# Hybrid attention/MoE layer on one core: the second tile of x is loaded through ScalarE's DMA queue

## What is computed

```python
def rms_norm(x, w):
    y = x * rsqrt(mean(x * x, axis=-1, keepdims=True) + 1e-5)
    return y * w
xn = rms_norm(h, ln1_w)          # h = x, [256, 1024]
proj = xn @ w_in                 # w_in [1024, 8720]
```

## Time and profile before

| | us |
|---|---|
| median of 3 runs (1234.31 to 1234.85) | 1234.81 |
| profiled execution, its own time | 1236.09 |
| its span, first to last instruction | 1234.3 |
| PE busy | 1156.1 (94%) |
| DVE busy | 389.9 (32%) |
| ACT busy | 240.8 (20%) |

### The profile page before, as it was taken

The page is one execution under the profiler, slowest core; times in us unless marked ns, Lnnn a source line. Parts: engine busy times, 40 slices in busy tenths (PEclk is TensorE's granted clock), DMA queues, the critical chain, the costliest instruction groups (busy, mean ns, idle before and its releaser), DMA issues.

```text
span 1234.3 us, 16298 instructions
## 1 busy us (share of the span) xinstructions
PE 1156.1 (94%) x6999; PEld 586.7 (48%) x6999; DVE 389.9 (32%) x674; ACT 240.8 (20%) x340; POOL 8.5 (1%) x26
## 2 busy tenths in 40 slices
PE   9999999999999999989889898989898989898997
PEld 8888888888633343333333333333333333333332
DVE  7775647656521221211111111212111112111112
ACT  6334446544410000100000000001000100000002
POOL 2000000000000000000000000000000000000000
PEclk9999999999999999999999999999999999999999
DMA  8745333496999999999999999999999999999996
GB/s 272 257 148 201 137 136 137 145 410 230 403 429 418 435 431 427 433 430 433 432 431 433 429 433 431 433 433 429 433 430 433 432 431 433 429 433 429 426 423 277
DMA packets 48029, 456.95 MB, mean 370 GB/s; under 512 B 5780, under 2 KB 5928, under 8 KB 32088
## 3 DMA queue, kind: packets, MB, share of 16 engines
q1 hardware_dynamic: 47832, 456.14, 88.8%
q10 hardware_dynamic: 160, 0.27, 0.1%
HBM read 455.35 MB, written 1.05 MB: 370 GB/s over the span
## 4 chain that ended last, share of the span: by engine, by line
PE 60%; DMA 37%; DVE 1%; SPq 0%; ACT 0%; issue 0%; DVEq 0%; ACTq 0%
PE ps L1492 58%; DMA ring<-in_w_up_dram 22%; DMA arena<-in_w_up_dram 13%; DMA ring<-in_w_down_dram 2%; PE ps L2019 1%; DMA ring<-in_w_in_dram 1%; DVE w_split L974 0%; PE ps L1903 0%; SPq L595 0%; ACT w_split L676 0%; PE ps L1686 0%; PE ps L1801 0%; PE ps L1650 0%; PE ps L1792 0%; DVE h_sb L1483 0%
## 5 line engine op out<-in xcount | busy, mean ns | idle before, releaser
L1492 PE MATMUL ps<-ring,arena 128*64 128x512 f32 x2304 | 523.0, 606 | 48.8 <-DMA ring<-in_w_up_dram 47.3
L1492 PEld LDWEIGHTS ps<-ring,arena 128*64 128x64 f32 x2304 | 163.2, 139 | 378.5 <-issue 298.4
L1492 PE MATMUL ps<-arena 128*64 128x512 f32 (+4 forms) x964 | 198.0, 544 | 18.1 <-DMA arena<-in_w_up_dram 18.1
L1411 DVE TENSOR_SCALAR arena<-ps 128x512 f32<-128x512 f32 x32 | 22.1, 692 | 485.0 <-PE ps L1492 485.0
L1492 PEld LDWEIGHTS ps<-arena 128*64 128x64 f32 (+1 forms) x964 | 74.3, 145 | 129.4 <-issue 99.7
L974 DVE TENSOR_TENSOR w_split<-ring,w_split 128x2048 fp32r<-128x2048 f32 x48 | 109.7, 2291 | 78.1 <-ACT w_split L676 78.0
L873 ACT ACTIVATE arena<-arena 128x512 f32<-128x512 f32 x32 | 20.2, 631 | 549.9 <-DVE arena L1411 549.9
L1492 PE MATMUL ps<-w_split,x_split 128*128 128x512 f32 x528 | 123.7, 393 | 0.0
L676 ACT ACTIVATE w_split<-ring 128x2048 fp32r<-128x2048 f32 x47 | 89.6, 1913 | 105.0 <-PE ps L1492 93.8
L1492 PEld LDWEIGHTS ps<-w_split,x_split 128*128 128x128 f32 x528 | 98.9, 189 | 20.7 <-issue 0.5
L1492 PE MATMUL ps<-x_split,w_split 128*128 128x256 f32 (+1 forms) x544 | 93.2, 331 | 2.4 <-DVE arena L1201 1.3
(11 more groups left out here) (250 smaller groups left out, 592.4 us busy)
## 6 DMA issues: line engine op xcount, KB each, us to landing
ring<-in_w_up_dram SPq DMA_DIRECT2D x38, 4096.0 KB, 31.1
ring<-in_w_down_dram SPq DMA_DIRECT2D x19, 4096.0 KB, 30.0
arena<-in_w_up_dram SPq DMA_DIRECT2D x12, 4096.0 KB, 31.1
ring<-in_w_in_dram SPq DMA_DIRECT2D x17, 2048.0 KB, 7.8
ring<-in_w_up_dram SPq DMA_DIRECT2D x16, 2048.0 KB, 11.5
arena<-in_w_down_dram SPq DMA_DIRECT2D x7, 4096.0 KB, 29.8
arena<-in_w_up_dram SPq DMA_DIRECT2D x6, 2048.0 KB, 15.6
ring<-in_w_down_dram SPq DMA_DIRECT2D x6, 2048.0 KB, 18.5
```

Source lines behind the costliest of these rows:

```text
L1411: dve.tensor_scalar(glu_c, ps[bank][:, :], LIMIT, None, ALU.min).then_inc(glu_ok, 1)
L1492: return pe.matmul(dst, lhsT, rhs, start=start, stop=stop, skip_group_check=True)
```

## The change

SP issues tile 0 of x only and goes straight on to the weights. Tile 1 of x is issued by ACT on its own queue, behind the norm's weights and a wait for `early_ok`, and so ahead of ACT's table load. The wait for `early_ok` that was there stays where it was. Nothing else differs: the same bytes go to the same places, and the same semaphore `x_in[1]` tells of the landing.

```diff
         @block.sync
         def _(sp):
-            for t in range(TT):
-                sp.dma_start(h_sb[:, t, :], x[0, t * P:t * P + P, :]).then_inc(x_in[t], 16)
+            sp.dma_start(h_sb[:, 0, :], x[0, 0:P, :]).then_inc(x_in[0], 16)
...
         @block.scalar
         def _(act):
             act.dma_start(ln1_r, ln1_w[0].rearrange("(k p) -> k p", p=P)).then_inc(ln1_in, 16)
+            act.wait_ge(early_ok, 2)
+            act.dma_start(h_sb[:, 1, :], x[0, P:SEQ, :]).then_inc(x_in[1], 16)
 
             act.wait_ge(early_ok, 2)
             act.activation(warm[:, 0:1], epsc[:, 0:1], ACT.Sqrt)
```

## The result

| | before | after |
|---|---|---|
| median us, 15 runs each | 1234.31 (1233.50 to 1236.15) | 1236.46 (1234.91 to 1238.08) |
| profiled execution, own time / span | 1236.09 / 1234.3 | 1237.26 / 1235.5 |
| start of the long PE run | 13.21 | 15.95 |
| start of the experts' first chain step | 320.20 | 322.98 |

The ratio of the times is 1.0018, with a 95% interval of 1.0011 to 1.0026: the change costs 2.2 us. The forecast was 1234.8 in a range up to 1236.0, so the range was missed by 0.46, and "no change" was wrong as a mechanism, though the loss lies just inside the 0.2% that was counted as no change.

What follows compares the result with a forecast made beforehand. The prediction took the landing of the first megabyte of weights to bound the start, passed on one to one. Weights -0.1 and x +0.1 summed to 0, giving a median of 1234.8 us, range 1233.9 to 1236.0.

Steps and rivals of the forecast that it cites:

- no change: Whole kernel: -0.1 for the weights and +0.1 for x sum to 0, median 1234.8; chance 0.51.
- What bounds the kernel, and a shift goes through one to one: Kernel start: the first megabyte of weights bounds it, and any shift there moves everything behind it equally.
- SP's issues move up: First weights: issued 0.46 us earlier without tile 1's issue, landing 0.1 earlier, bounds 0 to 0.46.
- Tile 1 is issued by ACT: ACT's start: tile 1 issued at about 1.45, 0.2 us later; table load, over by 3.4, covered by tile 0's wait.
- The two tiles share the engines: Load of x: alternating queues land tile 0 0.75 us late (bounds 0 to 1.0), tile 1 0 to 0.5 late.
- x has 0.92 in hand: Before the first weight matmuls: delaying x by D costs D - 0.92, nothing below that; D forecast 0.75 to 0.87.
- x as the bound: Rival at the start: tile 0 1.0 or tile 1 over 0.9 late, cost 0.3 to 1.0, about 1235.4; chance 0.14.
- the clock at 1.75: Rival at the start: PE idles before the first diagonal and its clock falls, cost 1.75, 1236.6; chance 0.04.
- The idle of 1.4 us: PE, in the clock rival: idle from about 5.3 to 6.7 before the first diagonal, where it was 0.60.
- the rival of the starved queue: ACT's queue served behind SP's backlog: x 13.2 us late, kernel 12.3 slower, 1247.1; chance 0.03.
- The rival that I built on that rule: Start: engines finish tile 0's packets first, D under 0.5, weights gain 0.2 to 0.46, 1234.4; chance 0.27.

Runs made afterwards that it cites:

- 30 fillers: Changed kernel with 30 instead of 2 small filler matmuls on PE between the two tiles' products: 1235.58 us, ratio to the kernel before 1.0011.
- 24: Changed kernel with 24 instead of 2 small filler matmuls on PE between the two tiles' products: 1235.36 us, ratio to the kernel before 1.0010.
- changed kernel, second profile: Changed kernel measured again with nothing altered: 1236.05 us, ratio to the kernel before 1.0017; profiled execution's own time 1234.80.
- late tile, filled: Kernel before with four DVE memsets ahead of tile 1's squares, plus 30 instead of 2 PE fillers between the tiles' products: 1235.49 us, ratio 1.0013.
- third profile: Changed kernel, nothing altered, profiled a third time in a single execution: 1235.85 us.
- late tile unfilled: Kernel before with four DVE memsets between tile 0's diagonal and tile 1's squares, DMA order untouched: 1236.71 us, ratio 1.0019.
- the filler run: Kernel before with 80 filler matmuls on PE ahead of the first products with weights: 1237.96 us, ratio 1.0029.
- second profile of before: Kernel before measured again with nothing altered, against itself: 1234.36 us, ratio 0.9996.
- both tiles were issued together: Changed kernel with ACT issuing tile 1 before the norm's weights, at about 0.82, when SP issues tile 0: 1235.66 us, ratio to the kernel before 1.0008.

## Why the prediction was wrong

**Tile 1's diagonal sets the start.** The start of tile 1's diagonal on DVE and the start of the run stand in one relation wherever x is the bound and the clock holds: 8.41 and 13.36 (30 fillers), 9.00 and 13.95 (24), 8.70 and 13.66 (changed kernel, second profile), 8.96 and 13.91 (late tile, filled). The difference is 4.95 or 4.96 each time. With the clock down it is 7.21, 5.97 and 6.02 (changed kernel, first and third profile; late tile unfilled). So the price of the clock in the start is 2.3 us, 1.0, 1.1 or, once, 0. Without it the changed kernel would start at 8.74 + 4.95 = 13.7, 0.5 to 1.0 behind the kernel before.

How the loss of 2.2 us divides is measured best by the late tile alone, filled and unfilled beside the kernel before: median spans of 1233.5, 1235.0 and 1232.4, so 1.1 for the late tile and 1.5 for the clock. For the change itself it is an estimate: 0.5 to 1.0 for the late tile as just worked out, and the rest, 1.2 to 1.7, for the clock. Only three executions of the changed kernel show their clock (2.3, 0 and 1.0, a mean of 1.1). The median spans agree: that of the changed kernel is 1234.3 beside 1232.4 for the kernel before, 1.9 more, and with 30 fillers it is 0.7 more.

**The steps of the prediction.**

- *What bounds the kernel, and a shift goes through one to one*: right. 2.74 at the run is 2.78 at the experts in the profiles, and the filler run lost all it was delayed by. In the first pair of profiles only 1.2 of it is left at the end, because the profiled execution of before was a long one: its experts' part took 1234.3 - 320.2 = 914.1, its second profile 912.9, and those of the changed kernel 912.5, 912.3 and 912.8. Over all 13 profiles the dense part, from the run to the experts, lasted 306.6 to 307.1 us and the experts' part 912.3 to 914.1, in no order of the start: nothing behind the start swallows a shift, but the experts' part moves by 1.8 us of its own accord.
- *SP's issues move up, worth 0.1*: the bound was wrong, though nothing hung on it. I took the share of 0.98 as proof that the engines could carry no more. They were occupied, but moved 311 GB/s; at a share of 1.02 it was 364 in the second profile of before and 383 in the changed kernel. Against my 0 to 0.46 the weights came 1.4 to 1.7 us earlier than in the first profile of before, and 0.8 to 1.2 earlier than in its second.
- *Tile 1 is issued by ACT, at 1.45, the table load is covered*: right (1.47; warm by 3.4).
- *The two tiles share the engines; tile 0 is 0.75 late, tile 1 0 to 0.5*: this is **the step that failed**. I let tile 1 begin 0.95 us after its issue, from a queue that had nothing before it. It began at about 4.4, 2.9 us after its issue, behind some 16 pieces per engine of the earlier queue, so tile 0 was not late at all and tile 1 was 1.7 late. In even sharing by pieces I was right, but 2.0 us too early. Sharing as I had drawn it did take place where both tiles were issued together; there tile 0 was 1.5 late, twice my 0.75.
- *x has 0.92 in hand*: short by 0.3 for the profile that I read. By the relation above x alone would have let the run begin at 7.03 + 4.95 = 11.98, so it had 13.21 - 11.98 = 1.23 in hand, and 1.71 late less 1.23 gives the 0.5 seen from 13.21 to 13.7. I had left out that with x as the bound the breaks inside the first 16 matmuls close up (2.15 us with 30 fillers, for 2.56) and the transposes behind them take 0.87 and not 1.09. In the second profile of before, where the weights were earlier, x had 0.86 in hand (6.87 + 4.95 = 11.82, the run at 12.68).
- *Rivals*: two came true in their effect, x as the bound at 0.3 to 1.0 and the clock at 1.75. I gave them 0.14 and 0.04 as if one excluded the other. But the same late tile makes both. Together they give 0.3 + 1.75 to 1.0 + 1.75, that is 2.1 to 2.8, and the loss is 2.2; that this fits is partly luck. The 1.75 came from 32 matmuls in the experts, and in the start the clock cost 2.3, 0 and 1.0. The idle of 1.4 us was forecast for the wait before tile 0's diagonal, which was 0.48; the clock fell at the wait before tile 1's, 1.87. And tile 1 was late because it started late, which the rival of the starved queue (0.03) had in its mechanism, though with 13.2 us and not 1.7.

The Trainium skill, "DMA: Bandwidth & Descriptors", section "Queues, rings and completion order", says that an engine drains a packet of several descriptors from one row before it turns to another. The start of the second queue, after some 16 pieces per engine, could be such a packet, but where both tiles were issued together it came after 2.5 per engine, so these runs do not settle it. The steady state, 94 packets against 91 of the same size, is even sharing over the whole stretch, and these counts cannot tell in how small portions. The rival that I built on that rule (tile 0 in time, weights earlier) was right in both its observations, and wrong in its sign, as it left tile 1 where it had been.

**Open.** Why the engines move some 16 pieces first where SP's queue is 0.2 to 0.7 us ahead, and whether the number depends on the size of a piece, was not tried; all of these were 4 KB or 2 KB. Why the clock fell in some executions and held in others with nearly the same wait is not explained, nor what sets the moment of its first rise. What adds up to 1 us outside the span with 24 or 30 fillers between the tiles, and not with 80 further down, is not explained either.

## What to carry to other kernels

A second queue is not a second path. In these runs what it was given, 0.2 to 0.7 us after the other queue's first issues, started only when that queue had moved some 16 pieces per engine, and from then on took its share of the same engines. So give it what is needed later, not what is needed next, unless a run shows otherwise, and put the transfer that something waits for at the head of the queue that was filled first. When a wait in front of TensorE grows, price the clock together with the wait: here the two were one event, not two rivals. And a busy share of the DMA engines near 1 was no proof here that they could carry no more.

## What was not expected of the hardware

- An issue on ACT's queue at 1.47 moved its first packet at about 4.4 us; one at 0.82 at about 2.75. They landed 5.9 and 5.1 us after their issues. What the other queue had been given by then counted, and not the queue alone.
- With two queues in use the same engines moved more at nearly the same busy share. From 5.6 to 8.0 us it was 311 to 364 GB/s (share 0.96 to 1.02) in the five profiles that load x and the first weights by SP's queue alone, and 381 to 408 (1.02 to 1.05) in the eight that use both. The size of the pieces is not the reason, since it was 381 and 392 where the two queues shared weights, in 2 KB pieces. Why it is so is not shown. The hole from 4.6 to 5.6 varies by itself: 193 to 289 GB/s in the five.
- After an idle of 1.87 to 1.96 us, soon after PE had first become busy, the clock fell in three profiles (two of the changed kernel and the late tile unfilled) and not in a fourth with 1.82. Twice it fell during the idle, and in the late tile unfilled only when PE was at work again (granted clock 1.00 from 8 to 9, 0.94 from 9 to 10, 0.50 behind it). Neither the idle of 1.01 in the kernel before nor one of 1.59 with both weight pieces on ACT's queue brought it down.
